# A DeltaNet head loop: context tiles dealt first, sums of weights for two pairs early, another order of convolution taps

## What is computed

```python
h = rmsnorm(x, norm1_g) * (1 + scale1) + shift1
proj = h @ w_in                      # pool, q, k, v, gate, beta, alpha, merge columns
a_out = pool_mixer(proj[..., :OFF_Q], ...) @ pool_proj
b_in, s_f, s_b = deltanet_mixer(proj, ...)     # 8 heads of width 128, two directions
mixed = merge[..., :D] * a_out + merge[..., D:] * (b_in @ dn_proj)
x = x + gate1 * (mixed @ w_out)
x = x + gate2 * expert_choice_ffn(rmsnorm(x, norm2_g) * (1 + scale2) + shift2, ...)

# deltanet_mixer, per head
q, k, v = silu(short_conv(q)), silu(short_conv(k)), silu(short_conv(v))   # 5 taps
q, k = l2norm(q) * 128 ** -0.5, l2norm(k)
# chunks: triangular solve with lower(k k^T * decay * beta), then a scan over the chunks
o = rmsnorm(o_forward + flip(o_backward)) * onorm_g * silu(gate)
```

## Time and profile before

| | us |
|---|---|
| median of 3 runs | 2573.36 |
| lowest, highest | 2573.13, 2573.65 |
| the profiled execution | 2571.28 |
| its span | 2569.5 |
| mean granted TensorE clock | 0.968 |

### The profile page before, as it was taken

How to read it: one execution, slowest core, us unless ns; L and a number is a source line. 1 busy time by engine, 2 the same in 40 slices (tenths; PEclk the granted TensorE clock), 3 DMA queues, 4 the chain that set the end, 5 groups by cost and what they waited for, 6 DMA issues and landing times.

```text
span 2569.5 us, 39903 instructions
## 1 busy us (share of the span) xinstructions
PE 2370.0 (92%) x14256; PEld 1718.9 (67%) x14256; DVE 1122.5 (44%) x2133; ACT 943.5 (37%) x2447; POOL 440.5 (17%) x295
## 2 busy tenths in 40 slices
PE   6889899898989989897999999959999999999998
PEld 3456556465655556565564444549999999999996
DVE  2657585765758576674623531770100100010013
ACT  3154555536455553644431113312223223222313
POOL 0222231322323132232310000000110011011000
PEclk8989999999999999998999999979999999999999
DMA  9610202011010201102224332266788788878874
GB/s 325 233 44 20 65 26 73 17 39 58 21 65 25 74 17 39 44 10 65 68 94 173 112 130 98 91 220 217 237 285 300 251 276 289 292 239 287 298 246 157
DMA packets 198401, 361.05 MB, mean 141 GB/s; under 512 B 8954, under 2 KB 72327, under 8 KB 195243
## 3 DMA queue, kind: packets, MB, share of 16 engines
q1 hardware_dynamic: 192139, 341.77, 38.0%
q0 software_dynamic: 6176, 18.29, 2.8%
HBM read 319.97 MB, written 40.06 MB: 140 GB/s over the span
## 4 chain that ended last, share of the span: by engine, by line
PE 52%; DVE 2%; issue 1%; DMA 1%; ACT 1%; POOL 0%; SPq 0%; DVEq 0%; ACTq 0%; POOLq 0%
PE bank L2373 20%; PE bank L2387 10%; PE bank L2002 5%; PE bank L1739 4%; PE bank L729 3%; PE bank L1757 2%; PE bank L710 1%; PE bank L2011 1%; PE bank L2345 1%; PE bank L2355 1%; PE bank L926 0%; PE bank L718 0%; DMA arena<-in_w_in 0%; PE bank L2413 0%; PE bank L995 0%
## 5 line engine op out<-in xcount | busy, mean ns | idle before, releaser
L729 PE MATMUL bank<-arena 128*128 128x512 f32 x1344 | 697.4, 622 | 21.6 <-ACT arena L763 21.6
L2373 PE MATMUL bank<-arena 128*128 128x144 f32 x4096 | 512.9, 286 | 3.1 <-ACT arena L2421 3.1
L2373 PEld LDWEIGHTS bank<-arena 128*128 128x128 f32 x4096 | 509.6, 190 | 3.2 <-ACT arena L2421 3.2
L2488 DVE TENSOR_TENSOR arena<-arena,bank 128x144 f32<-128x144 f32 x128 | 39.1, 306 | 698.2 <-ACT arena L2435 698.2
L729 PEld LDWEIGHTS bank<-arena 128*128 128x128 f32 x1344 | 221.9, 195 | 119.4 <-issue 95.0
L2387 PE MATMUL bank<-arena 128*128 128x144 f32 x2048 | 257.3, 286 | 0.7 <-DVE arena L2488 0.7
L2387 PEld LDWEIGHTS bank<-arena 128*128 128x128 f32 x2048 | 253.8, 189 | 1.9 <-DVE arena L2488 0.9
L1101 ACT ACTIVATE arena<-bank 128x384 f16<-128x384 f16 (+1 forms) x360 | 163.7, 492 | 215.1 <-PE bank L918 118.4
L2435 ACT ACTIVATE arena<-bank 128x144 f32<-128x144 f32 x128 | 37.4, 292 | 464.3 <-PE bank L2373 464.3
L926 PEld LDWEIGHTS bank<-arena 128*128 128x128 f16 x1296 | 98.7, 98 | 149.8 <-issue 127.4
L1186 DVE SCALAR_TENSOR_TENSOR arena<-arena 128x1156 f32<-128x1156 f32 x96 | 143.1, 1490 | 0.3
(11 more groups left out here) (311 smaller groups left out, 3185.2 us busy)
## 6 DMA issues: line engine op xcount, KB each, us to landing
arena<-in_exp_w_gate SPq DMA_DIRECT2D x32, 2048.0 KB, 10.1
arena<-in_exp_w_up SPq DMA_DIRECT2D x32, 2048.0 KB, 14.9
arena<-in_exp_w_down SPq DMA_DIRECT2D x32, 2048.0 KB, 10.8
arena<-in_w_in SPq DMA_DIRECT2D x52, 512.0 KB, 5.2
arena<-in_ada_w SPq DMA_DIRECT2D x24, 1024.0 KB, 7.9
side_dram<-arena SPq DMA_DIRECT2D x20, 576.0 KB, 5.7
arena<-g_dram SPq DMA_DIRECT2D x16, 576.0 KB, 4.3
arena<-in_x_sample SPq DMA_DIRECT2D x16, 512.0 KB, 7.1
```

The lines of the kernel that those rows point to most:

```text
L729: ins = nc.tensor.matmul(bank[:, 0:LH], w[:, k, :], x[:, k, :], start=(k == 0 and job[2] in "127"), stop=(k == KH - 1), skip_group_check=( ...
L2373: last = nc.tensor.matmul(banks[3 + f % 2][:, m * CAP:(m + 1) * CAP], w_unit[2 * half + m][:, k, col:col + P], xsT[:, k, :], start=(k == 0 ...
```

## The change

- Order: in a loop head the context jobs of q, v, k and the gate come first, then the rest of qv, kg, AB. In the last head `g2` moves behind the pair CD.
- Budgets: `start` 5 to 4, `Y20` 1.5 to 1, `Y21` 1.5 to 0.5, `Y22` 1 to 0.5, `P2_2`, `P4_2`, `P8_2` 1 to 0, `fix` 3 to 4, `end1` 4 to 5.5. By the code's arithmetic the units dealt to a loop head are then: start 4 (5 before), nk 2.75 (2), qT 3.25 (4), kk 4 (4), Y2 together 2 (4), `end1` and `end2` together 14 (9 before; one more unit, `scan8c`, stands just ahead of them in both). The last head keeps its own budgets but for the three P places; its three units go to `end2`.
- Sums: POOL makes the first sums of qv and of kg and the fourth of kg at the head's start, then the thirds; then the masks (1427); the fourth of qv comes behind the triangles' work (1434). kg gets three buffers of its own, which lie over masks and tables that are no longer read. In the last head the gate's sums come early.
- Convolution: v's taps come first (levels 16, 32, 64 and ahead of the scan), then q's, then k's; the scan steps 3 and 5 have two taps.
- ACT copies the jobs of `start` ahead of the silu of v, and no longer behind the wait for `scan_done`.
- The last head loads `w_dn[0]` behind CD's loads and stores. In the prologue the sum `h_sum3` (1484) waits for `scan_done`, and PE no longer waits for it.

```diff
+        silu_c = take(KD * (P // 4))
+        tab_words = take(9 * NT * 2 * H)
+        tab = {n: tab_words[:, i * NT * 2 * H:(i + 1) * NT * 2 * H].rearrange("p (t d) -> p t d", t=NT)
+               for i, n in enumerate(("g", "gc", "tmp", "tmp2", "beta", "gcb", "ndec", "kd", "dl"))}
...
+        SUMS_AT = MASKS_AT + 8 * P
+        w_sum2 = [arena[:, SUMS_AT + i * KH * P:SUMS_AT + (i + 1) * KH * P].rearrange("p (k n) -> p k n", k=KH) for i in range(3)]
...
-        ORDER = pair_jobs("qv") + pair_jobs("kg") + pair_jobs("AB")
-        ORDER_LAST = pair_jobs("AB") + ("g0", "g1", "g2") + pair_jobs("CD") + pair_jobs("EF")
+        (QV_C, QV_X), (KG_C, KG_X) = split("qv"), split("kg")
+        ORDER = QV_C + KG_C + QV_X + KG_X + pair_jobs("AB")
+        ORDER_LAST = pair_jobs("AB") + ("g0", "g1") + pair_jobs("CD") + ("g2",) + pair_jobs("EF")
...
-        FILL = {"start": 5, "nk": 2.75, "qT": 4, "kk": 4, "Y20": 1.5, "Y21": 1.5, "Y22": 1, "X0": 1, "X1": 1, "X2": 1, "res": 2, "fix": 3, "end1": 4}
-        FILL |= {f"{x}{b}_{g}": 1 for b in LEVELS for x in "ZP" for g in range(3)}
+        FILL = {"start": 4, "nk": 2.75, "qT": 4, "kk": 4, "Y20": 1, "Y21": 0.5, "Y22": 0.5, "X0": 1, "X1": 1, "X2": 1, "res": 2, "fix": 4, "end1": 5.5}
+        FILL |= {f"{x}{b}_{g}": 0 if b in LEVELS[:3] and (x, g) == ("P", 2) else 1 for b in LEVELS for x in "ZP" for g in range(3)}
...
-        CONV_TURN = (3, 0, 2, 1)
+        CONV_TURN = (3, 2, 0, 1)
+        CONV_TURN_FIRST = (3, 0, 2, 1)
...
+        SUMS = ("qv1", "qv2", "kg1", "kg2", "kg4", "qv3", "kg3", "qv4", "AB1", "AB2", "AB3", "AB4")
+        SUMS_LAST = ("AB1", "AB2", "g1", "g2", "AB3", "AB4", "CD1", "CD2", "CD3", "CD4", "EF1", "EF2", "EF3", "EF4")
...
 (SP, last head)
-            sp.wait_ge(sem("pj_filled"), job_at(h, ORDER_LAST, "g2"))
-            sp.dma_start(w_dn[0], ...).then_inc(sem("w_dn_in0"), 16)
             store_states(sp, h)
...
+            sp.wait_ge(sem("pj_filled"), job_at(h, ORDER_LAST, "g2"))
+            sp.dma_start(w_dn[0], ...).then_inc(sem("w_dn_in0"), 16)
...
 (ACT)
             silu(1)
             silu(0)
+            evac("start")
             silu(2)
...
             act.wait_ge(sem("scan_done"), h + 1)
-            evac("start")
...
 (DVE)
+            taps = [(j, tap) for j in (2, 0, 1) for tap in range(TAPS)]
...
                 add(f"P{b}_2")
-                if not last_h and lv > 0:
-                    conv_tap(dve, h + 1, 0, lv - 1)
+                if lv >= 3:
+                    tap()
...
-            taps = [(j, tap) for j in (2, 1) for tap in range(TAPS)]
+            tap()
             remainder(1)
             tap()
             state(0)
...
             for t in range(2, NT):
                 remainder(t)
                 tap()
+                if t in (3, 5):
+                    tap()
                 add(f"scan{t}b")
                 state(t)
-            if not last_h:
-                conv_tap(dve, h + 1, 1, TAPS - 1)
...
 (POOL)
-            sums_first(first, len(FIRST) + len(ORDER) * h)
-            sums_third(first)
-            sums_fourth(first)
+            pool.wait_ge(sem("pj_filled"), len(FIRST) + len(ORDER) * h)
+            if last_h:
+                sums_first("AB")
+                gate_sums()
+                sums_third("AB")
+            else:
+                sums_first("qv")
+                sums_first("kg")
+                sums_fourth("kg")
+                sums_third("qv")
+                sums_third("kg")
...
+            sums_fourth("AB" if last_h else "qv")
+            all_drained(pool, h, 1, "kq")
+            for d in range(2):
+                low_part(d)
+                attention(d)
...
 (prologue)
             pool.wait_ge(sem("pj_filled"), len(FIRST))
+            pool.wait_ge(sem("scan_done"), 1)
             nc.gpsimd.tensor_tensor(h_sum3, h22, h12, ALU.subtract).then_inc(sem("sums_ready"), 1)
...
-            pe.wait_ge(sem("sums_ready"), H_SUMS)
```

More of the change, by code:

```diff
@@ L131, in build @@
         conv_w = take(CONV_ROWS)
-        silu_c = take(KD * (P // 4))
         modT = take(2 * 48)
@@ L139, in build @@
         eps_c, qscale_c, one_c = small[:, 0:1], small[:, 1:2], small[:, 2:3]
-        tab = {n: take(NT * 2 * H).rearrange("p (t d) -> p t d", t=NT)
-               for n in ("beta", "gcb", "g", "gc", "ndec", "kd", "dl", "tmp", "tmp2")}
-        tab_words = arena[:, at_word[0] - 9 * NT * 2 * H:at_word[0]]
         PERSIST = at_word[0]
@@ L679, in weights_wait, with summed_at, sums_of @@
                 eng.wait_ge(sem(f"w_side_in{x % 2}"), 16 * (h + 1 + x // 2))
-        H_SUMS, W_SUMS = 4, 12
-        def sums_before(h, order, job):
-            pairs = [n for n in order if n[-2:] == "c1"]
-            mine = [n for n in pairs if n[:2] == job[:2]]
-            extra = 2 if order is ORDER_LAST and job[:2] in ("CD", "EF") else 0
-            return H_SUMS + W_SUMS * h + 4 * pairs.index(mine[0]) + extra
+        H_SUMS = 4
+        SUMS = ("qv1", "qv2", "kg1", "kg2", "kg4", "qv3", "kg3", "qv4", "AB1", "AB2", "AB3", "AB4")
+        SUMS_LAST = ("AB1", "AB2", "g1", "g2", "AB3", "AB4", "CD1", "CD2", "CD3", "CD4", "EF1", "EF2", "EF3", "EF4")
+        def summed_at(h, order, name):
+            return H_SUMS + len(SUMS) * h + (SUMS_LAST if order is ORDER_LAST else SUMS).index(name) + 1
+        def sums_of(pair):
+            one = weights_of(pair[0])
+            return w_sum2 if pair == "kg" else w_sum + [one[:, KH:KD, :]]
         def project(pe, h, order):
@@ L1169, in conv_tap @@
         def conv_tap(dve, h, j, tap):
+            first = isinstance(h, int) and h == 0
+            turn = (CONV_TURN_FIRST if first else CONV_TURN).index(j)
             if tap == 0:
-                if isinstance(h, int) and h == 0:
+                if first:
                     dve.wait_ge(sem("pj_drained"), copied_at(0, FIRST, ("q2", "k2", "v2")[j]))
@@ L1179, in conv_tap @@
             else:
[L1181 removed]
+                dve.wait_ge(sem("tap_done"), h * (3 * (TAPS - 1)) + (turn - 1) * (TAPS - 1) + tap)
             w = conv_w[:, bass.ds(tap * 3 * H + j * H + h, 1)]
@@ L1199, in add, with tap @@
                 added[0] = to
+            taps = [(j, tap) for j in (2, 0, 1) for tap in range(TAPS)]
+            def tap():
+                if not last_h:
+                    conv_tap(dve, h + 1, *taps.pop(0))
             def decay_arguments(d):
@@ L1334, in body_dve @@
                 tap()
+                if t in (3, 5):
+                    tap()
                 add(f"scan{t}b")
                 state(t)
-            if not last_h:
-                conv_tap(dve, h + 1, 1, TAPS - 1)
+            assert last_h or not taps
             add("end1")
@@ L1380, in body_pool, with sum_out, sums_first @@
             order = ORDER_LAST if last_h else ORDER
[L1382 to L1387 removed]
+            def sum_out(name, out, x, y, op):
+                if name[-1] in "24":
+                    pool.wait_ge(sem("sums_ready"), summed_at(h, order, name[:2] + {"2": "1", "4": "2"}[name[-1]]))
+                nc.gpsimd.tensor_tensor(out, x, y, op).then_inc(sem("sums_ready"), 1)
+            def sums_first(pair):
                 for name in pair:
                     weights_wait(pool, h, order, name)
[L1390 to L1394 removed]
+                one, two, to = weights_of(pair[0]), weights_of(pair[1]), sums_of(pair)
+                sum_out(pair + "1", to[0], two[:, 0:KH, :], two[:, KH:KD, :], ALU.add)
+                sum_out(pair + "2", to[1], to[0], one[:, 0:KH, :], ALU.subtract)
             def sums_third(pair):
@@ L1448, in attention @@
                 nc.gpsimd.tensor_tensor(attnT[d], kq[1], dm[d], ALU.mult).then_inc(sem("attn_ready"), 1)
-            if last_h:
-                gate_sums()
-            else:
-                sums_first(second, job_at(h, order, first + "5"))
-            all_drained(pool, h, 1, "kq")
-            low_part(0)
-            if not last_h:
-                sums_third(second)
-            attention(0)
-            if not last_h:
-                sums_fourth(second)
-            low_part(1)
-            attention(1)
-            if last_h:
-                sums_first(second, job_at(h, order, "g2"))
-                sums_third(second)
-                sums_fourth(second)
-            sums_first(third, job_at(h, order, second + "5"))
-            sums_third(third)
-            sums_fourth(third)
+            sums_fourth("AB" if last_h else "qv")
[3 more added lines that the diff above has]
+                attention(d)
+            if last_h:
+                for pair, used in (("CD", "AB5"), ("EF", "CD5")):
+                    pool.wait_ge(sem("pj_filled"), job_at(h, order, used))
+                    sums_first(pair)
+                    sums_third(pair)
+                    sums_fourth(pair)
+            else:
+                pool.wait_ge(sem("pj_filled"), job_at(h, order, "kg3"))
+                sums_first("AB")
+                sums_third("AB")
+                sums_fourth("AB")
             for d in range(2):
```

45 lines of the change are left out of this document (18 added, 27 removed).

## The result

The changed kernel takes **2438.84 us** (median of 4 runs, 2438.54 to 2439.22) against 2573.24 (2570.35 to 2573.65) for the kernel before: ratio 0.948, 95% interval 0.9464 to 0.9496. The profiled executions differ by 132.3 us of span.

The account below looks back on a forecast made before the run. PE, busy 92% of 2569.5 us, was taken as the bound, so only its waits and lower clock could yield time. The terms summed to 95.1 us, giving 2476.2 and, with 2.1 for the median, 2478; range 2445 to 2525.

Parts of the forecast that it names:

- (e): Levels: PE loses units but most slack stays; -0.2 us in seven heads, +0.9 in the last, together -0.5; bounds +22, -28.
- (b): Head start: context tiles and early copies cut 4.9 us of waits and slow clock to 1.5; -20.4 us over six heads.
- (c): Wait before the triangles: masks start 5.7 us sooner, 1.9 of 5.6 us left; together -30.7 us.
- (a): End of the head: 15 units instead of 10 cover the chain, the 1.32 us wait goes; -9.2 us over seven heads.
- (d): Clock behind the wait before the triangles: the slow stretch goes, 3.0 us in each of eight heads, -24.0 us.
- Last head: The forecast gain lying in the last head: 13.5 us.
- (f): Last head: g2's four units and scan work cover EFc0's 4.09 us wait for weights; -5.7 us, bounds 0 and -7.
- (g): Prologue: line 1484 moved behind the head's start frees some 4 us of DVE; -2.3 us (0 to -4).
- all goes: Rival: no waits left at head start and before triangles, half the levels' waits gone; 34 us better, 2444; chance 0.10.
- The levels lose: Rival: in levels 2 to 8 lost cover pulls the clock to 1.2 GHz; +126 against -95, 2604; chance 0.06.
- The start stays late: Rival: seven sums delay DVE, key norm 3 us late, wait before triangles near 5 us; 42 us back, 2520; chance 0.14.

Follow-up runs that it names:

- experiment 7: Changed kernel with the old budgets (start 5, Y2 4 units, all P places 1, fix 3, end1 4), all else kept: 2434.7 us.
- experiment 2: Kernel before with only the taps at their new places: 2566.8 us; both edits, with qv's fourth sum also behind masks and triangles' diagonal: 2506.4 us.
- experiment 9: Changed kernel with POOL's fourth sum of qv made to wait for the last merge of the levels' first step: 2435.7 us.
- experiment 6: Changed kernel with kg's four sums back behind qv's fourth, beside the triangles and levels; their own buffers stay: 2461.8 us.
- experiment 4: Changed kernel with all of qv's side jobs ahead of kg's, and kg's third sum behind qv's fourth: 2485.6 us.
- experiment 8: Changed kernel with POOL's last prologue sum (h_sum3) started without the wait for scan_done, as before: 2439.4 us.
- experiment 1: Kernel before with only POOL's fourth sum of the first pair moved behind the masks and the triangles' diagonal: 2518.1 us.
- experiment 5: Changed kernel with ACT's copy of the head's first side job put back behind scan_done and the third silu: 2444.4 us.
- experiment 3: Kernel before with qv's fourth sum and the taps moved, plus ACT's copy of the first side job ahead of its third silu: 2474.2 us.

## Why the prediction went wrong where it did

The mechanism was right, the sign too. The step that failed is the size of three terms of the sum: the levels (e), put at 0.2 us a loop head, gave 3.1 more than that; the head's start (b) was to leave 1.5 us of waiting and left none; the wait before the triangles (c) was to leave 1.9 and left 0.85. In b and c I had charged counter-costs that did not arise or were smaller; in e I had let far too little of the old waits go.

- (a) End of the head, 1.3 a head: the size came out, but by luck. The old budgets leave 0.18 there (experiment 7), and the moved taps alone take the waits from 9.2 to 1.3 us over the run (experiment 2): the shorter chain did it, which the prediction did not name. Whether the added cover would have done it without the taps is not shown.
- (b) Head start, 3.4 a head, leaving 1.5: nothing is left. The nine decay arguments did take 6.18 us beside six sums, and ended 0.47 behind the sixth (397.95 + 7.73 = 405.68; 399.97 + 6.18 = 406.15). The Trainium skill (SBUF, State Buffer; section "Who interferes with whom") has the second instruction to come blocked until the first has ended, and this row agrees. Five of the nine took 0.70 to 1.31 us, each beside a sum, the other four 0.28. But my seventh sum waited for PE until 406.87, so DVE was ready 0.45 before ACT's key norm and not 0.9 after it. I had counted POOL's operations in a row and not asked what each waits for.
- (c) Before the triangles, leaving 1.9: 0.85 is left. The two copies of line 1245, which I let the masks hold up, took 1.41 us with the masks beside them, against 1.40 alone.
- (d) The clock: 3.0 a head forecast, 2.8 measured in the triangles. Right, though 3.0 was the loss of the head read; in the other loop heads before, 2.4 to 3.1 us were lost there. Over the whole run the busy time shows more, 38.5 us, because the start's clock came back too (its 1.7 stood in b).
- (e) The levels, 0.2 a head: 3.3. This is the largest miss, some 22 of 37 us. I had put the slow merges down to DVE's own chain, so that 1 us of 3.5 would go, and expected 0.9 of new waits from the units taken away. In the head shown all of the 3.5 went and 0.85 came (0.26 and 0.59). But these 0.85 belong to qv's fourth sum beside a merge: once it is out of the way they are gone, with the new budgets kept (experiment 9). The merges' means (lines 1264 and 1269) tell the same: 776 and 715 ns before, 667 and 567 after, 594 and 558 with the old budgets. The same section of the Trainium skill has a DVE instruction with two inputs in SBUF contend with a GpSimd instruction that reads SBUF. The merges of lines 1286 and 1291 are held up in just this way; I had applied the rule to the decay arguments and the tap and not to them. Experiment 6 gives the price back, and merge 1279, one of whose inputs is a bank, took 0.55 in the midst of an attention step (experiment 4).
- Last head, 13.5 forecast: 11.4. The waits of c and f did go; the new 2.43 for CD's sums and a new 1.04 for DVE (line 787) were not foreseen. (f) itself held: `g2` covers EFc0's load.
- (g) Prologue 2.3: 1.8 at head 0's first job, of which the sum's place kept between 0.6 and 2.1 to the end (experiment 8).
- Of the rivals, "all goes" (2444) comes nearest, and even it let half of the level waits stand. The range, said to take it in, began at 2445, and it left out e's own bound of -28. "The levels lose" is refuted: no clock below 1.00 in the levels of the head shown, and the loop heads' mean is 1.00. "The start stays late" is refuted by the key norm.

What stays open: how much of the last step (2474 to 2439) is the sums' place and how much the order. Experiments 4 and 6 each undo one and cost 47 and 23 us, more together than the step, because each leaves POOL waiting on PE or adding beside merges. The step also holds the changes in the prologue and the last head, which went from 162.5 to 159.3 us. Putting only qv's fourth sum back ahead of the masks in the changed kernel was not tried: it waits for job qv2, which is dealt behind the triangles there, and these need the masks.

## What to carry to other kernels

On an engine that works in order, look for the instruction that waits on the bottleneck engine, and ask what is queued behind it: one 1.3 us addition here cost 53 us. When two elementwise engines run together, read the durations of the shorter operations against their free duration; where one is stretched, place the other in a gap by having it released by the first one's last operation. And price a stall of PE together with the clock behind it.

## What the runs showed of the hardware

- A predicated copy of 128x384 with both operands in SBUF (0.56 us alone) that starts beside a POOL tensor_tensor ends about 0.42 us behind the end of that one; it took up to 2.58 us (experiments 4, 6 and 9). The form that reads a bank is not held up: 0.55 us (experiment 4). The hold-up goes the other way too: in the changed kernel POOL's attention step of the second direction, begun beside a tap that DVE had begun first (`457.84 1.42`, unstretched), took 3.74 us; that of the first direction, with no tap beside it, took 2.63.
- POOL's masks (affine_select) did not hold up DVE's float16 copies: 1.41 us with (changed kernel) and 1.40 (experiment 1), 1.40 without (kernel before).
- The granted clock: behind a wait of 3.73 us it was 0.70 over 9.6 us (experiment 2, both edits; 1.4 to 3.1 us lost by head), behind one of 2.45 us that followed one of 1.24 it was 0.59 over 5.0 us (experiment 4), behind the last head's 2.43 us 0.79 over 8.2 us. Behind waits of 1.60 (experiment 5) and 1.11 us (experiment 3) it stayed at 1.00. Behind the pair of 1.19 us in experiment 6 it did so in four loop heads, and fell in two, to 0.88 over 14 us in one.
